# Moving small steps within the hand-written order of a float32 decoder layer: square sum, rotary, attention and weight-difference steps

## The chip, the cores and the metric

The kernel runs on one core of a Trainium2 chip. A core has five engines that each work through their own queue of instructions in order: TensorE (PE in the profile, with PEld for its weight loads), VectorE (DVE), ScalarE (ACT), GpSimd (POOL) and SyncE (SP), which here issues most transfers. They are tied together by semaphores only. The metric is device time of one execution in microseconds (us); the change is judged by the median of several executions against the kernel before.

## The reference: what is computed

One decoder layer in float32 on 520 rows: 512 of a prompt and 8 single rows of a sample group that has its own caches. d_model is 2048, the hidden width of the feed-forward 5632.

```python
h = rmsnorm(x, g_mix_pre)
proj = h @ w_in                          # q | k | v | B | C | u | gate_a | gate_b
a = attention(rope(q), rope(k), v)       # window 128, 16 heads over 2 key heads, a sink per head
b_out = cb * dwconv3(cc * cu)
merged = sigmoid(ga + b0) * (a @ w_attn_branch) + sigmoid(gb + b1) * (b_out @ w_conv_branch)
x = x + rmsnorm(merged @ w_o, g_mix_post)
up, gt = split(rmsnorm(x, g_ffn_pre) @ w_ffn_up)
x = x + rmsnorm((gelu(dwconv3(up) + bias) * gt) @ w_ffn_down, g_ffn_post)
x = x + sigmoid(x @ w_ple_gate) * (p @ w_ple)
```

## The kernel before

Activations lie feature-major: 128 features on the partitions, 520 rows along the free side in two halves of 260. A projection is worked off in **units**. A unit makes a 2 by 2 block of results (two column tiles of 128, two halves of 260 rows) with seven products in place of eight, in the manner of Strassen and Winograd: the weights and the rows enter as sums and differences of blocks. There are 116 units in seven **sets**: units 0 to 31 are the input projection (in it 2 to 5 are q, 6 to 17 the convolution's C, u and B, 18 to 31 gates), 32 to 39 w_o, 40 to 83 the up projection, 84 to 107 the down projection in three sets, 108 to 115 the last gate. Between the input projection and w_o stand the two branch projections (L967 to L999), and between w_o and the up projection the p projection.

**Float32 out of a faster type.** In the first unit of a set (`first_unit`, L866) TensorE multiplies float32 directly. In all others (`unit`, L897) each product is made of three matmuls in the reduced type float32r: high times high, high times low, low times high. A product j (0 to 6) has two halves h, so a unit has 14 **steps** i = 2j + h. For each step ScalarE writes the high part of the weights (`v_hi`, L1063) and VectorE the low part (`v_lo`, L1656), into a ring of four slots. Both run four steps ahead of TensorE: ScalarE's high part for step i + 4 waits until TensorE has used step i (`v_used`).

**VectorE's order.** `unit` at L1794 is one loop over the 14 steps. In step i it issues, in this order: the low part for step i + 4; in the second unit of a set (the one after `first_unit`) at i = 0, 3, 5, 8 two low parts of the rows (`o_low`, L1742); at i = 4 and 5 the weight difference s4; at 8 and 9 s1 and at 10 and 11 s3 of the next unit's weights; at 12 and 13 s2; then the set's own work, `evac(u, i)`. At i = 9 alone `evac` stands ahead of the rest. `evac` holds, for every set, the three adds of `sums` (L1822): at 7 the add "c11" after product 3, at 9 the add "c22" (L1831) after product 4, at 11 the add "c12" after product 5. It also holds the work of the stage: rotary (`sine`, `cosine`, `turn_q`), the convolution, attention of the prompt (`masked`, `shifts`, `probabilities`, `attention_out`) and of the sample rows (`sample_max` to `sample_out`).

**What TensorE waits for.** Product 6 accumulates in the bank that c22 reads, so it waits for c22 (`banks_free`, L849, j = 6). Each step waits for its low part. `between(u)` (L820) places TensorE's small work in a unit: key -1 is ahead of product 0, key j behind product j. That is `rotate` (the rotary matmul; both rotations of a unit use one bank, so the second waits for the first one's `sine`), `turn` (transposes of the probabilities), `scores`, `values`, and the same for the sample rows. Attention of the prompt runs in 16 parts; unit u in `ATT` scores and exponentiates a part, unit u in `TURN` transposes it and multiplies it with v. Units 19 to 30 do both, and gate units also take a sigmoid at i = 0 and 1.

**The start.** ScalarE squares each of the 16 row blocks and scales it (L1042, L1044), VectorE sums the squares into `sqacc1` (L1449). TensorE makes k and v from the scaled rows as they come (L724). The sum over partitions is two matmuls with a matrix of ones (`square_sum`, L707); from it VectorE and ScalarE make the inverse root (L1438, L1441, L1035), VectorE scales all row blocks with it (`h_row`, L1455) and builds the first differences (t1, s1, s3, t2, s2), and unit 0 can go on.

Of the kernel before, what the change touches and what calls it, by code (L numbers as in the profile page):

```python
# [8 lines left out]
KD = D // P  # L9
TP, TS = 512, 8  # L10
T = TP + TS
HALF = T // 2
# [13 lines left out]
U_O, N_O = 32, KD // 2  # L26
# [56 lines left out]
def build(nc, sstream, x_in, p_in, chan_in, sinkp_in, sinks_in, cstate_in, fstate_in,  # L83
# [5 lines left out]
    with ExitStack() as ctx:  # L89
# [610 lines left out]
        def _(pe):  # L700
# [3 lines left out]
            def x_half(k, h):  # L704
                return raw4[:, 2 * (k // KH) + h, k % KH, :]

            def square_sum():  # L707

                pe.wait_ge(sq_added, KD - 1)
                pe.wait_ge(pool_set, 3)  # L710
                for h in range(2):
                    mm = pe.matmul(pair[1][:, h, 0:HALF], ones[:, :],
                                   sqacc1[:, h * HALF:(h + 1) * HALF], start=True, stop=True)
                mm.then_inc(sum_ready, 1)

            for k in range(KD):
                if k == KD - 4:
                    square_sum()
                pe.wait_ge(x_rdy, k + 1)
                for n, w in enumerate(quarter_of(k)[:2]):  # L720
                    if k % KH == 0:
                        pe.wait_ge(s_rdy[0][2 * n + k // KH], 16)
                    for h in range(2):
                        mm = pe.matmul(pair[2 + n][:, h, 0:HALF], w[:, quarter_of(k)[2]], x_half(k, h),  # L724
                                       start=k == 0, stop=k == KD - 1, skip_group_check=True)
                mm.then_inc(kv_used, 1)
            def rotate(r):

                u = U_Q + r // 2
                if r < KA:  # L730
                    for n in ((c11_out, c12_out), (c22_out, c21_out))[r % 2]:
                        pe.wait_ge(n, u + 1)
                    src = d_h[u % 2][:, r % 2, :]
                else:
                    src = k_in
                pe.wait_ge(kv_out, 2)
                if r:
                    pe.wait_ge(rope_sin, r)
                for h in range(2):
                    mm = pe.matmul(pair[2][:, h, 0:HALF], rotm[:, :],  # L740
                                   src[:, h * HALF:(h + 1) * HALF], start=True, stop=True)
                mm.then_inc(rope_rot, 1)
# [77 lines left out]
            def between(u):  # L820

                if u - 1 in range(U_Q, U_CONV):
                    r = 2 * (u - 1 - U_Q)
                    return {-1: lambda: rotate(r), 1: lambda: rotate(r + 1)}
                if u == U_CONV + 1:
                    return {0: v_turn, 1: lambda: rotate(KA)}
                if u == U_CONV + 3:
                    return {0: sample_scores}
                if u == U_CONV + 4:
                    return {-1: sample_turn, 3: sample_values}  # L830
                here = {}
                if u in TURN or u in ATT:
                    here[-1] = lambda: (turn(TURN[u]) if u in TURN else None,
                                        scores(ATT[u]) if u in ATT else None)
                if u in TURN:
                    here[2] = lambda: values(TURN[u])
                if u == LAST:
                    here[4] = lambda: turn(ATT[u])
                    here[5] = lambda: values(ATT[u])
                return here  # L840
# [578 lines left out]
        def _(dve):  # L1419
# [374 lines left out]
            def unit(u, evac, last):  # L1794

                n = s_of(u, 0)
                ahead = 16 if u == U_O - 1 else 14 if last and u != U_UP - 1 else 18
                for i in range(14):
                    if i == 9:
                        evac(u, i)  # L1800
                    if i + 4 < ahead:
                        v_low(n + i + 4)
                    if is_first(u - 1) and i in (0, 3, 5, 8):
                        o_low(set_of(u), {0: 3, 3: 4, 5: 5, 8: 6}[i])
                    if i in (4, 5):
                        s4(u, i - 4)
                    if i in (8, 9) and u not in (U_O - 1, U_UP - 1):
                        s1(u + 1, i - 8)
                    if i in (10, 11) and u not in (U_O - 1, U_UP - 1):
                        s3(u + 1, i - 10)  # L1810
                    if i in (12, 13) and not last:
                        s2(u + 1, i - 12)
                    if i != 9:
                        evac(u, i)

            def by(s, evac, first=None):
                u0, n, _ = SETS[s]
# [69 lines left out]
            def h_evac(u, i):  # L1887
                d, k = d_h[u % 2], kind(u)
                if U_Q < u <= U_CONV:
# [4 lines left out]
                        cosine(r)  # L1894
                    if i == 2:
                        turn_q(r)
                    if i == 3:
                        sine(r + 1)
                        cosine(r + 1)
                    if i == 6:  # L1900
                        turn_q(r + 1)
# [38 lines left out]
                    if i == 8:  # L1940
                        sample_prob()
                if u == U_CONV + 4:
                    if i == 1:
                        sample_turned()
                    if i == 8:
                        sample_out()
                if u in ATT:
                    if i in (0, 1):
# [2 lines left out]
                        shifts(ATT[u])  # L1951
                    if i == 6:
                        probabilities(ATT[u])
                if u in TURN and i == 7:
                    attention_out(TURN[u])
                if u == LAST and i == 12:
                    attention_out(ATT[u])
# [390 lines left out]
```

## Time and profile before

| | before |
|---|---|
| median of 3 runs | 2798.61 us (2797.02 to 2798.67) |
| the profiled execution: its own time | 2798.67 us |
| its span, first to last instruction | 2796.1 us |
| TensorE busy | 2697.9 us |
| VectorE busy | 2294.1 us |
| ScalarE busy | 1416.9 us |
| mean granted TensorE clock | 0.987 |

The span is what the trace covers; 2.6 us of the execution lie around it. Busy times overlap, so they don't add up. TensorE's matmuls are pipelined: one of the 128x260 matmuls takes 0.28 us from start to end, but the next one starts 0.12 us later. In the same way the next VectorE operation on 128x512 elements starts 0.60 us after one that lasts 0.68 us. Intervals below are from start to start where a queue is full.

### The profile page before, as it was taken

How to read it: one execution, taken by the hardware profiler on the slowest of the kernel's cores; microseconds unless marked ns; L12 is line 12 of the kernel's file. 1: busy time of each engine (PE TensorE's matmuls, PEld its weight loads, DVE VectorE, ACT ScalarE, POOL GpSimd, SP SyncE). 2: the span in 40 equal slices, each digit the busy share in tenths (PEclk: the TensorE clock that was granted, in tenths of full speed). 3: DMA queues.
4: the chain of work that ended last, by engine and by line, in shares of the span. 5: the costliest groups of instructions: out<-in, count | busy, mean ns of one | idle time of the engine just before them, and what ended most of it. 6: DMA issues, size and time to landing. Idle time of an engine off the chain costs nothing. (4 is left out here: it accounts for less than half of the span.)

```text
span 2796.1 us, 55643 instructions
## 1 busy us (share of the span) xinstructions
PE 2697.9 (96%) x21199; PEld 2619.9 (94%) x21199; DVE 2294.1 (82%) x4039; ACT 1416.9 (51%) x2511; POOL 30.3 (1%) x52
## 2 busy tenths in 40 slices
PE   7999999999999999989999999999999999999799
PEld 6999999999999989879999999999998999989599
DVE  6988888777754598798888888888888788899988
ACT  5444455666652255545555555555554454445354
POOL 0000000000000000000000000000000000000000
PEclk9999999999999999999999999999999999999799
DMA  5333333333353422542323233333334342425343
GB/s 187 133 127 115 107 115 113 116 122 125 116 175 136 162 91 90 196 150 102 135 102 130 107 123 115 116 122 109 129 106 160 119 153 91 140 85 171 123 186 123
DMA packets 119157, 357.89 MB, mean 128 GB/s; under 512 B 13097, under 2 KB 37297, under 8 KB 116384
## 3 DMA queue, kind: packets, MB, share of 16 engines
q1 hardware_dynamic: 116944, 350.19, 35.6%
q0 software_dynamic: 2048, 5.68, 0.6%
q8 instruction: 82, 1.34, 0.2%
q14 instruction: 83, 0.68, 0.1%
HBM read 311.74 MB, written 45.32 MB: 128 GB/s over the span
## 5 line engine op out<-in xcount | busy, mean ns | idle before, releaser
L915 PE MATMUL pair<-o_hi,v_hi 128*128 128x260 f32 x6006 | 1715.0, 286 | 39.5 <-DVE v_lo L1656 11.7
L915 PE MATMUL pair<-o_hi,v_lo 128*128 128x260 f32 x6006 | 1699.2, 283 | 0.0
L1063 ACT ACTIVATE v_hi<-s_raw 128x512 fp32r<-128x512 f32 (+1 forms) x1380 | 855.3, 625 | 1008.1 <-PE pair L915 824.5
L915 PE MATMUL pair<-lo,v_hi 128*128 128x260 f32 x4290 | 1215.3, 283 | 0.0
L1656 DVE TENSOR_TENSOR v_lo<-s_raw,v_hi 128x512 fp32r<-128x512 f32 (+1 forms) x1380 | 934.5, 681 | 333.6 <-ACT v_hi L1063 285.7
L915 PEld LDWEIGHTS pair<-o_hi,v_hi 128*128 128x128 f32 x6006 | 1133.0, 189 | 64.3 <-issue 32.3
L915 PEld LDWEIGHTS pair<-o_hi,v_lo 128*128 128x128 f32 x6006 | 1135.1, 189 | 0.0
L915 PEld LDWEIGHTS pair<-lo,v_hi 128*128 128x128 f32 x4290 | 809.8, 189 | 0.3
L915 PE MATMUL pair<-lo_E,v_hi 128*128 128x260 f32 x858 | 243.2, 283 | 0.0
L915 PE MATMUL pair<-lo_A,v_hi 128*128 128x260 f32 x858 | 241.9, 282 | 0.0
L1063 ACT ACTIVATE v_hi<-s_one 128x512 fp32r<-128x512 f32 (+1 forms) x218 | 135.9, 626 | 192.8 <-PE pair L915 187.0
L915 PEld LDWEIGHTS pair<-lo_E,v_hi 128*128 128x128 f32 x858 | 161.6, 188 | 0.1
L915 PEld LDWEIGHTS pair<-lo_A,v_hi 128*128 128x128 f32 x858 | 161.3, 188 | 0.0
L1703 DVE TENSOR_TENSOR s_raw<-s_raw,s_raw 128x512 f32<-128x512 f32 (+1 forms) x232 | 156.0, 675 | 0.0
L1676 DVE TENSOR_TENSOR s_one<-s_raw,s_raw 128x512 f32<-128x512 f32 (+1 forms) x232 | 155.8, 675 | 0.0
L1684 DVE TENSOR_TENSOR s_raw<-s_raw,s_raw 128x512 f32<-128x512 f32 (+1 forms) x232 | 155.2, 674 | 0.0
L1694 DVE TENSOR_TENSOR s_raw<-s_one,s_raw 128x512 f32<-128x512 f32 (+1 forms) x232 | 155.1, 674 | 0.0
L1656 DVE TENSOR_TENSOR v_lo<-s_one,v_hi 128x512 fp32r<-128x512 f32 (+1 forms) x218 | 146.7, 675 | 5.2 <-ACT v_hi L1063 1.8
L892 PE MATMUL pair<-raw,s_raw 128*128 128x260 f32 x508 | 116.5, 385 | 5.0 <-DVE y_sb L1831 1.8
L892 PEld LDWEIGHTS pair<-raw,s_raw 128*128 128x128 f32 x508 | 94.7, 190 | 24.0 <-issue 2.8
L987 PE MATMUL pair<-br_hi,v_lo 128*128 128x260 f32 x512 | 103.2, 283 | 0.0
L987 PE MATMUL pair<-br_lo,v_hi 128*128 128x260 f32 x512 | 103.0, 283 | 0.0
(209 smaller groups left out, 2077.8 us busy)
## 6 DMA issues: line engine op xcount, KB each, us to landing
s_raw<-in_sstream SPq DMA_DIRECT2D x472, 512.0 KB, 4.7
s_raw<-in_sstream SPq DMA_DIRECT2D x32, 384.0 KB, 3.4
f_scr<-fo SPq DMA_DIRECT2D x88, 130.0 KB, 1.8
g_scr<-d_h SPq DMA_DIRECT2D x16, 520.0 KB, 2.7
g_in<-g_scr SPq DMA_DIRECT2D x32, 260.0 KB, 2.7
x_scr<-y_sb SPq DMA_DIRECT2D x8, 1040.0 KB, 3.9
raw<-f_scr SPq DMA_DIRECT2D x7, 1040.0 KB, 4.9
raw<-in_x SPq DMA_DIRECT2D x4, 1040.0 KB, 6.4
```

Source lines behind the costliest of these rows:

```text
L892: mm = pe.matmul(out, w[:, kk * P:kk * P + P], src[:, k, :], start=j in (0, 1, 3) and k == 0, stop=k == nk - 1, skip_group_check=True)
L915: mm = pe.matmul(out, wt[:, slot, kk * P:kk * P + P], r[:, k, :], start=j in (0, 1, 3) and k == 0 and n == 0, stop=k == nk - 1 and n == 2, ...
L987: mm = pe.matmul(pair[2 + p][:, half, 0:HALF], wt[:, slot, kk * P:kk * P + P], r[:, k, half * HALF:(half + 1) * HALF], start=k == 0 and i ...
L1063: nc.scalar.activation(v_hi[:, n % 4, 0:width], src, ACT.Copy).then_inc(v_hi_rdy, 1)
L1656: dve.tensor_tensor(v_lo[:, n % 4, 0:width], src, v_hi[:, n % 4, 0:width].bitcast(f32), ALU.subtract).then_inc(v_lo_rdy, 1)
L1676: dve.tensor_tensor(w_src(u, 1, h), quarter(u, 2, h), quarter(u, 3, h), ALU.add)\
L1684: dve.tensor_tensor(quarter(u, 2, h), quarter(u, 0, h), quarter(u, 2, h), ALU.subtract)\
L1694: dve.tensor_tensor(quarter(u, 0, h), w_src(u, 1, h), quarter(u, 0, h), ALU.subtract)\
L1703: dve.tensor_tensor(quarter(u, 1, h), quarter(u, 1, h), quarter(u, 0, h), ALU.subtract)\
```

## The change

Five edits. The square sum goes behind the k and v matmuls of all 16 row blocks. The second rotary matmul of a unit goes from behind product 1 to behind product 0, and its `sine` from step 3 to step 2. The sample rows' transposes go from the head of unit 10 to behind product 5 of unit 9, their value matmuls from behind product 3 to behind product 1 of unit 10, and the two copies on VectorE with them. The prompt's `values` go from behind product 2 to behind product 1, and `attention_out` from step 7 to step 5. In VectorE's loop s1 and s3 go one step ahead, and the special place of `evac` at step 9 goes away: it follows the low part and s3 there, as in all other steps.

```diff
-            def square_sum():
-                pe.wait_ge(sq_added, KD - 1)
-                ...
             for k in range(KD):
-                if k == KD - 4:
-                    square_sum()
                 pe.wait_ge(x_rdy, k + 1)
...
+            pe.wait_ge(sq_added, KD - 1)
+            pe.wait_ge(pool_set, 3)
+            for h in range(2):
+                mm = pe.matmul(pair[1][:, h, 0:HALF], ones[:, :],
+                               sqacc1[:, h * HALF:(h + 1) * HALF], start=True, stop=True)
+            mm.then_inc(sum_ready, 1)
...
-                    return {-1: lambda: rotate(r), 1: lambda: rotate(r + 1)}
+                    return {-1: lambda: rotate(r), 0: lambda: rotate(r + 1)}
...
-                    return {0: sample_scores}
+                    return {0: sample_scores, 5: sample_turn}
                 if u == U_CONV + 4:
-                    return {-1: sample_turn, 3: sample_values}
+                    return {1: sample_values}
...
-                    here[2] = lambda: values(TURN[u])
+                    here[1] = lambda: values(TURN[u])
...
                 for i in range(14):
-                    if i == 9:
-                        evac(u, i)
                     if i + 4 < ahead:
                         v_low(n + i + 4)
...
-                    if i in (8, 9) and u not in (U_O - 1, U_UP - 1):
-                        s1(u + 1, i - 8)
-                    if i in (10, 11) and u not in (U_O - 1, U_UP - 1):
-                        s3(u + 1, i - 10)
+                    if i in (7, 8) and u not in (U_O - 1, U_UP - 1):
+                        s1(u + 1, i - 7)
+                    if i in (9, 10) and u not in (U_O - 1, U_UP - 1):
+                        s3(u + 1, i - 9)
                     if i in (12, 13) and not last:
                         s2(u + 1, i - 12)
-                    if i != 9:
-                        evac(u, i)
+                    evac(u, i)
...
                     if i == 2:
                         turn_q(r)
+                        sine(r + 1)
                     if i == 3:
-                        sine(r + 1)
                         cosine(r + 1)
...
                 if u == U_CONV + 4:
-                    if i == 1:
+                    if i == 0:
                         sample_turned()
-                    if i == 8:
+                    if i == 4:
                         sample_out()
...
-                if u in TURN and i == 7:
+                if u in TURN and i == 5:
                     attention_out(TURN[u])
```

## Rows read from the trace of the kernel before

**Rows 1.** The page's busy times: us, share of the span, instructions.

```profile
PE 2697.9 (96%) x21199; PEld 2619.9 (94%) x21199; DVE 2294.1 (82%) x4039; ACT 1416.9 (51%) x2511; POOL 30.3 (1%) x52
```

**Rows 2.** TensorE's waits by releaser: us in total, times, longest us.

```profile
PE pair L915 <- DVE v_lo L1656: 11.7, 9, 4.4
PE pair L915 <- DVE d_h L1831: 9.5, 14, 2.4
PE pair L915 <- DVE y_sb L1831: 5.0, 4, 2.0
PE pair L915 <- DVE g_half L1831: 2.4, 1, 2.4
PE pair L915 <- DVE d_sb L1831: 1.3, 1, 1.3
```

**Rows 3.** Timeline of the start: start us, us, engine, line, operation, [idle before].

```profile
26.48 0.70 DVE L1449 TENSOR_TENSOR sqacc<-sqacc,sq_a 128x520 f32<-128x520 f32 x1 [0.45 <-ACT sq_a L1042]
...
31.57 1.04 PE L712 MATMUL pair<-sqacc,ones 128*128 128x260 f32 x4
...
32.45 7.18 PE L724 MATMUL pair<-raw,s_raw 128*128 128x260 f32 x32
32.65 0.70 DVE L1438 TENSOR_SCALAR nv_a<-pair 128x520 f32<-128x520 f32 x1 [5.46 <-PE pair L712]
...
45.54 3.77 PE L892 MATMUL pair<-raw,s_one 128*128 128x260 f32 x16 [2.32 <-DVE s_one L1676]
```

**Rows 4.** Timeline of unit 26, an attention unit in the gates, three engines.

```profile
643.56 0.63 ACT L1063 ACTIVATE v_hi<-s_raw 128x512 fp32r<-128x512 f32 x1 [2.94 <-PE pair L915]
...
647.55 1.07 ACT L1205 ACTIVATE pT_sb<-pair 128x512 f32<-128x512 f32 x2
...
647.70 0.39 PE L915 MATMUL pair<-o_hi,v_hi 128*128 128x260 f32 x1
...
653.97 0.69 DVE L1656 TENSOR_TENSOR v_lo<-s_raw,v_hi 128x512 fp32r<-128x512 f32 x1 [3.03 <-ACT v_hi L1063]
...
660.41 0.68 DVE L1676 TENSOR_TENSOR s_one<-s_raw,s_raw 128x512 f32<-128x512 f32 x1
661.01 0.42 DVE L1831 TENSOR_TENSOR d_h<-pair,d_h 128x260 f32<-128x260 f32 x1
661.35 0.68 DVE L1656 TENSOR_TENSOR v_lo<-s_raw,v_hi 128x512 fp32r<-128x512 f32 x1
...
661.48 0.39 PE L915 MATMUL pair<-o_hi,v_hi 128*128 128x260 f32 x1 [0.44 <-DVE d_h L1831]
```

**Rows 5.** Timeline of unit 54, in the up projection: steps 9 to 12.

```profile
1512.77 0.63 ACT L1063 ACTIVATE v_hi<-s_raw 128x512 fp32r<-128x512 f32 x1 [0.81 <-PE pair L915]
...
1513.21 0.42 DVE L1831 TENSOR_TENSOR g_half<-pair,g_half 128x260 f32<-128x260 f32 x1
...
1515.45 0.29 PE L915 MATMUL pair<-o_hi,v_hi 128*128 128x260 f32 x1
```

**Rows 6.** Timeline of unit 4, with rotary: product 1's first matmul, the first sine.

```profile
145.50 0.28 PE L915 MATMUL pair<-o_hi,v_hi 128*128 128x260 f32 x1
...
145.55 0.69 DVE L1483 TENSOR_TENSOR rope_s<-pair,sin 128x520 f32<-128x520 f32 x1
```

**Rows 7.** Timeline of unit 13: the add c22 and product 6's first matmul.

```profile
354.50 0.42 DVE L1831 TENSOR_TENSOR d_h<-pair,d_h 128x260 f32<-128x260 f32 x1
...
355.61 0.29 PE L915 MATMUL pair<-o_hi,v_hi 128*128 128x260 f32 x1
```

**Rows 8.** Timeline of unit 9, the sample rows' scores: step 8's low part, product 6.

```profile
267.79 0.69 DVE L1656 TENSOR_TENSOR v_lo<-s_raw,v_hi 128x512 fp32r<-128x512 f32 x1 [1.41 <-ACT v_hi L1063]
...
271.21 0.39 PE L915 MATMUL pair<-o_hi,v_hi 128*128 128x260 f32 x1 [2.42 <-DVE d_h L1831]
```

**Rows 9.** Timeline of unit 31, the last with attention: transposes behind product 4.

```profile
783.11 1.06 PE L806 MATMUL pair<-ident,s_sb 128*128 128x128 f32 x8 [1.79 <-DVE a_st L1598]
```

**Rows 10.** Windows: us, busy us (instructions) of PE, PEld, DVE, ACT, POOL; clock, DMA, GB/s.

```profile
1022.00:1027.00 5.00, 4.82 (x28) 4.83 (x29) 5.00 (x11) 1.52 (x3) 0.00 (x0) 0.67 0.31 119
```

More of the change, by code:

```diff
@@ L705, in x_half @@
                 return raw4[:, 2 * (k // KH) + h, k % KH, :]
-            def square_sum():
-                pe.wait_ge(sq_added, KD - 1)
[L710 to L714, printed above, removed]
             for k in range(KD):
-                if k == KD - 4:
-                    square_sum()
                 pe.wait_ge(x_rdy, k + 1)
```

## The prediction

> **What bounds the kernel now.** I read the page's busy times first: TensorE is busy for 2697.9 of 2796.1 us [rows 1]. So at most 98 us can be won, and whatever makes TensorE wait inside a unit is paid in full, unless it takes the place of another wait. Then TensorE's waits by releaser [rows 2]. What the reader is to see: beside the low parts (v_lo) it is one small add, c22 at L1831, that TensorE waits for in 14 + 4 + 1 + 1 = 20 units, 18.2 us together. Product 6 needs that add. Then the timelines of single units, with one question: how long before product 6's first matmul does c22 end (its slack)? I made that difference for all 109 units that aren't the first of a set. In units 18 to 30 it is 0.05, and also in 1, 9, 33, 41, 85, 93, 101 and 109 (up to 0.13): there the add decides. It is 0.69 to 1.15 in 2, 7, 13 and 16 [rows 7], about 1.1 in the six shorter units 102 to 107, and 1.66 to 2.25 in 77 others, of which [rows 5] is one: 1515.45 less 1513.21 + 0.42. Unit 31 has 4.1. Everything in the change that touches VectorE's steps 7 to 9 has to be held against this list.
>
> **The c22 add at step 9.** Before, VectorE does in steps 7 to 9: low part, c11; low part, s1; c22. After: low part, s1, c11; low part, s1; low part, s3; c22. So three operations on 128x512 stand ahead of c22 that stood behind it: one s1, one low part and one s3. A step from s1 to c22 takes 661.01 - 660.41 = 0.60 us [rows 4], and each of the three has this size: 3 x 0.60 = 1.8 us later, where VectorE's queue is full. The total work of VectorE is unchanged; only the add comes later.
>
> Units 18 to 30. VectorE is full from the low part at 653.97 to the add [rows 4]; it started there because ScalarE released it, and ScalarE's own chain starts at 643.56, when TensorE has used step 0. So c22 comes a fixed time after step 0 of its own unit, and TensorE waits on it: 13 x 1.8 = 23.4 us. (Unit 18's wait isn't in the list of waits, but its product 6 starts 0.06 after the add like the others.)
>
> Units 13 and 16, 2 and 7. VectorE is full there too, but c22 ended 0.69, 0.69, 1.08 and 1.15 us early; for unit 13 that is 355.61 - 354.92 [rows 7]. The wait is 1.8 less the slack plus the 0.05 that a released matmul needs: 1.2 + 1.2 + 0.8 + 0.7 = 3.9 us.
>
> Second units of the sets. 1, 33, 41, 85 and 109 wait on c22 already, with VectorE full behind the low parts of the rows: 5 x 1.8 = 9.0 us. In 93 and 101 VectorE idled 0.99 and 0.79 us behind c11, which takes in the early s1: 1.2 and 0.9 (operations of 0.47 there); and in 101 a later wait of 0.6 on VectorE goes, since VectorE is no later than before: 1.6 together. In unit 9 the idle 1.41 us [rows 8] takes in the s1 as well: 1.2.
>
> The 77 units with slack. There VectorE isn't full, and c22 is bound by the high part for step 13, which ends at 1512.77 + 0.63 = 1513.40 [rows 5]. Low part and s3 (0.60 each), then the add of 0.42: 1515.02 to 1515.07, against a need at 1515.45. Some 0.4 is left (0.2 in the tightest), so these cost nothing. That cover is thin: where it is missed by 0.1 in all 77, it is 8 us. In 102 to 107 the same sum ends within 0.05 of the need; I take 0, and 0.1 each as a bound. s1 one step earlier also waits for its weights earlier. SP issues the last quarter of them behind the low part of step 13 of the unit before the last, nearly a unit ahead, so neither that nor SP's own wait shows.
>
> **The values behind product 1.** They wait for both copies of the transposed probabilities. These end at 647.55 + 1.07 = 648.62, while product 1 is through at 647.70 [rows 4]: TensorE would stand 0.95 us, with products 2 to 6 queued behind. In units 19 to 30 this isn't added. c22 is tied to step 0, and TensorE runs into its wait at product 6 anyway; the 0.95 is taken from that wait, which would be 0.44 + 1.8. Step for step nothing in ScalarE's chain asks for products 2 and 3 sooner. In units 14 and 17 (no sigmoid, slack 1.66) nothing swallows it: the copies end 0.73 us late, 2 x 0.75 = 1.5 us. `attention_out` at step 5 finds its matmuls done and costs nothing by itself. In unit 31 it is a gain: the transposes behind product 4 waited 1.79 for it [rows 9], and now wait for the probabilities, which end one low part and one copy sooner and start one copy later: -0.6, after the 0.95 is swallowed by the same wait.
>
> **The second rotation behind product 0.** It needs the first `sine` out of its bank. Product 0 ends where product 1 starts, 145.50; the sine ends at 145.55 + 0.69 = 146.24 [rows 6]. TensorE stands 0.8 us, in units 3 to 6: 3.2 us. The sine moved to step 2 makes a later operation of VectorE earlier, which nobody waited for.
>
> **The sample rows.** ss_prob is ready before c22 in unit 9, so the four transposes fall into TensorE's wait there, and unit 10 loses them: about -0.4. With the 1.2 above, unit 9 and 10 cost +0.8. The value matmuls only change place, their copy is ready.
>
> **The square sum.** The sum of squares is there at 26.48 + 0.70 = 27.2, but TensorE is behind and reaches the place at 31.57 [rows 3], so no wait is removed. After, the 32 matmul instructions of row blocks 12 to 15 stand ahead of it, 7.0 us from start to start of what follows. L1438 starts at 32.65, when the sum is out, with all of VectorE's start behind it (inverse root, row scaling, s1). TensorE already waits on that chain: 2.32 us for s_one at 45.54, with the k and v matmuls done long before [rows 3]. So the four blocks hid the inverse root, and after nothing does: +7.0 us.
>
> **The sum.** 23.4 + 3.9 + 9.0 + 1.6 + 1.5 - 0.6 + 3.2 + 0.8 + 7.0 = 49.8 us.
>
> **The clock.** In unit 33 a wait of 1.97 us (the longest of the y_sb row [rows 2]) was followed by a window with a granted clock of 0.67, a mix of full and the lower of the two levels (2.4 and 1.2 GHz) [rows 10]; the unit and the next took 1.65 us more than their like. Unit 9 with 2.42 and unit 31 with 1.79 saw no fall. Eight places (1, 9 and the second units) now wait longer: between 0 and 8 x 1.65 = 13 us; I take three, 5 us, since like waits before fell in some and not in others.
>
> Against the execution's own 2798.67 us (its span and 2.6 around it; the median is 0.06 less) this is 2798.7 + 49.8 + 5 = 2853.5 us.
>
> **The rivals.**
>
> *The clock falls in every attention unit.* After, these units have two waits, 0.95 and 1.25, every 26.5 us. If one of them drops the clock each time, 13 x 1.65 = 21 us come on top: 2875. Against it: 12 waits of 0.44 and one of 1.79 left the clock at full. The Trainium skill, page "TensorE: Matmul & The Clock Gate", section "HAM oscillation — how this bites in real kernels", says that a loop that waits in each turn can go back to half rate in each turn, and that half of the throttled time is lost. No stretch of this trace repeats such a fall. Chance 0.07.
>
> *The thin cover tears.* If the low part or s3 at step 9 takes 0.3 us more than I read off, the 77 units wait 0.3 each past their 0.4, or the first part of that: up to 23 us, 2876. For it: only 0.2 to 0.4 is left. Against: VectorE's times repeat to 0.02. Chance 0.08.
>
> *The add isn't what holds product 6.* The releaser is inferred. If product 6 waited for something else that ends near c22, such as its own low part, the add could slip without a price: what stays is 7.0 + 3.2 + 1.5, with a wait or two: 2811. Against it: a slack of 0.05 in 13 units in a row. Chance 0.07.
>
> *Faster.* The low part for step 13 no longer stands behind the add and a step's s1. If TensorE's waits on low parts, 11.7 us [rows 2], all came from there, they would go, and if the idle time before s_one took in the late square sum, the kernel would be at 2787. It decides in a unit only where c22 has more than 1.8 us of slack and a low part has none. Against it: where TensorE waits for low parts, c22 has none either, and these waits stand ahead of step 13. Chance 0.03.
>
> **How the numbers follow.** The forecast has the other 0.75; with its own bounds (clock 0 to 13, the shorter units 0 to 0.6, ±3 for the readings off single rows) it spans 2845 to 2866. The range takes in most of the two rivals above and part of the one below: 2838 to 2872. A change under 0.2%, 5.6 us, can't be told from none. Slower 0.96, same 0.01, faster 0.03.
>
> **What would show it.** Right: TensorE's waits on L1831 grow from 18.2 to some 50 us, in units 18 to 30 the period goes from 24.7 to 26.5 us, and new waits appear on the copies of the probabilities (15 times, 0.75 to 0.95) and on the rotary sine (4 times, 0.8); L1438 starts near 39.7; the up projection keeps its period of 20.17. Wrong: a period in the up projection above 20.2, attention units at 24.7 or above 27, or an L1438 that starts before 35.

## The result, and the profile after

The changed kernel takes 2859.39 us (median of four runs, 2858.37 to 2863.52), the kernel before 2797.82 us (four runs, 2795.78 to 2798.67). The ratio is 1.0224, with a 95% interval of 1.0206 to 1.0242: slower by 61.6 us. The forecast was 2853.5 us in a range of 2838 to 2872, and slower. The profiled execution after took 2858.77 us, with a span of 2856.3 us and a mean granted clock of 0.980. So the span grew by 60.2 us.

The page's busy times after, beside [rows 1]:

```profile
PE 2711.4 (95%) x21199; PEld 2633.2 (92%) x21199; DVE 2300.2 (81%) x4039; ACT 1418.6 (50%) x2511; POOL 30.3 (1%) x52
```

The number of instructions is the same on every engine. TensorE is busy 2711.4 - 2697.9 = 13.5 us longer with the same 21199 matmuls, and idle for the other 60.2 - 13.5 = 46.7 us. This isn't the split into clock and waits, for which the forecast had 5 and 49.8: a matmul at the lower clock counts as busy, but so do small stands between matmuls, and these changed as well (see `x3_values`). In units 18 to 30 the busy time grew by 318.68 - 313.93 = 4.75 us, although the clock cost 9.1 us there. The split is made below from the starts of the units.

TensorE's waits by releaser after, beside [rows 2] (c11, c22 and c12 now lie seven lines higher, the square sum's matmuls are at L719, the other lines below have moved up by three, four or seven):

```profile
PE pair L911 <- DVE d_h L1824: 31.2, 19, 3.6
PE pair L811 <- ACT pT_sb L1201: 12.3, 16, 0.8
...
PE pair L911 <- DVE v_lo L1652: 11.8, 9, 4.5
...
PE pair L911 <- DVE y_sb L1824: 9.6, 5, 3.8
...
PE pair L888 <- DVE raw L1451: 5.7, 1, 5.7
...
PE pair L911 <- DVE g_half L1824: 4.2, 1, 4.2
PE pair L911 <- DVE d_sb L1824: 3.1, 1, 3.1
PE pair L736 <- DVE rope_s L1479: 2.9, 4, 0.7
...
PE pair L764 <- DVE ss_sb L1539: 2.1, 1, 2.1
```

The waits on c22 (L1824) are 31.2 + 9.6 + 4.2 + 3.1 = 48.1 us, from 18.2. The waits on low parts are what they were, 11.8 after 11.7. New are the waits on the copies of the probabilities (16, 0.8 at most; before there was one of 0.3), on the rotary sine (4, 0.7), on the sample rows' probabilities (2.1) and on the scaled rows in unit 0 (5.7).

Timeline of the start, beside [rows 3], and of units 4, 9 and 13, beside [rows 6 to 8]:

```profile
26.60 0.70 DVE L1445 TENSOR_TENSOR sqacc<-sqacc,sq_a 128x520 f32<-128x520 f32 x1 [0.44 <-ACT sq_a L1038]
...
37.52 1.04 PE L719 MATMUL pair<-sqacc,ones 128*128 128x260 f32 x4
...
38.59 0.70 DVE L1434 TENSOR_SCALAR nv_a<-pair 128x520 f32<-128x520 f32 x1 [11.29 <-PE pair L719]
...
51.49 3.77 PE L888 MATMUL pair<-raw,s_one 128*128 128x260 f32 x16 [1.28 <-DVE s_one L1672]
...
155.70 0.69 DVE L1479 TENSOR_TENSOR rope_s<-pair,sin 128x520 f32<-128x520 f32 x1
...
156.54 1.12 PE L736 MATMUL pair<-d_h,rotm 128*128 128x260 f32 x4 [0.72 <-DVE rope_s L1479]
...
284.91 0.58 PE L764 MATMUL pair<-ident,ss_sb 104*128 104x104 f32 x4 [2.08 <-DVE ss_sb L1539]
...
286.45 0.39 PE L911 MATMUL pair<-o_hi,v_hi 128*128 128x260 f32 x1 [0.96 <-DVE d_h L1824]
...
372.87 0.42 DVE L1824 TENSOR_TENSOR d_h<-pair,d_h 128x260 f32<-128x260 f32 x1
...
373.34 0.39 PE L911 MATMUL pair<-o_hi,v_hi 128*128 128x260 f32 x1 [1.01 <-DVE d_h L1824]
```

VectorE now stands 11.29 us for the square sum, with the squares added up at 27.3. The inverse root begins at 38.59 in place of 32.65, and the rest of the start with it: TensorE works on s_one at 51.49, before at 45.54. In unit 4 TensorE stands for the sine. In unit 9 it stands for the sample rows' probabilities, and then once more for c22. In unit 13 product 6 starts 0.05 after the add, where it had 0.69 to spare.

Timeline of unit 26, beside [rows 4]. It starts at 682.87, the next one at 709.37:

```profile
684.61 0.63 ACT L1059 ACTIVATE v_hi<-s_raw 128x512 fp32r<-128x512 f32 x1 [2.95 <-PE pair L911]
...
688.60 1.07 ACT L1201 ACTIVATE pT_sb<-pair 128x512 f32<-128x512 f32 x2
...
689.72 1.09 PE L811 MATMUL pair<-pT_sb,v_tok 128*64 128x256 f32 x8 [0.82 <-ACT pT_sb L1201]
...
695.02 0.69 DVE L1652 TENSOR_TENSOR v_lo<-s_raw,v_hi 128x512 fp32r<-128x512 f32 x1 [3.04 <-ACT v_hi L1059]
...
702.06 0.68 DVE L1672 TENSOR_TENSOR s_one<-s_raw,s_raw 128x512 f32<-128x512 f32 x1
702.66 0.68 DVE L1652 TENSOR_TENSOR v_lo<-s_raw,v_hi 128x512 fp32r<-128x512 f32 x1
703.26 0.68 DVE L1680 TENSOR_TENSOR s_raw<-s_raw,s_raw 128x512 f32<-128x512 f32 x1
703.87 0.42 DVE L1824 TENSOR_TENSOR d_h<-pair,d_h 128x260 f32<-128x260 f32 x1
...
704.34 0.39 PE L911 MATMUL pair<-o_hi,v_hi 128*128 128x260 f32 x1 [1.78 <-DVE d_h L1824]
```

From the high part of ScalarE to c22 it is 703.87 - 684.61 = 19.26 us; in [rows 4] it is 661.01 - 643.56 = 17.45. The difference is 1.81, the three operations. One sees them in the order forecast: s1, low part, s3, add. The copies end at 689.67 and the values wait 0.82 for them. The wait on c22 is 1.78, which is 0.46 less than 0.44 + 1.8: the values' wait has been taken out of it in part, and `x3_values` shows where the rest of it went.

Timeline of the next unit, 27, TensorE from product 6 on:

```profile
730.83 0.39 PE L911 MATMUL pair<-o_hi,v_hi 128*128 128x260 f32 x1 [1.80 <-DVE d_h L1824]
...
731.65 0.42 PE L911 MATMUL pair<-o_hi,v_lo 128*128 128x260 f32 x1
731.87 0.42 PE L911 MATMUL pair<-o_hi,v_hi 128*128 128x260 f32 x1
...
734.69 0.33 PE L911 MATMUL pair<-lo,v_hi 128*128 128x260 f32 x1
```

Windows after (us, busy PE, PEld, DVE, ACT, POOL, clock, DMA share, GB/s): unit 26, unit 27, a stretch behind product 6's start in unit 27, units 18 to 30 together, and 40 units of the up projection:

```profile
682.87:709.37 26.50, 23.89 (x195) 22.43 (x193) 18.72 (x42) 16.17 (x32) 1.42 (x2) 1.00 0.31 110
709.37:737.38 28.01, 25.39 (x195) 23.93 (x193) 18.71 (x42) 16.17 (x32) 1.42 (x2) 0.94 0.30 105
...
731.00:734.50 3.50, 3.50 (x19) 3.50 (x20) 2.35 (x5) 0.63 (x1) 0.00 (x0) 0.55 0.51 195
...
466.30:818.40 352.10, 318.68 (x2491) 300.09 (x2489) 246.43 (x540) 205.46 (x410) 17.58 (x25) 0.97 0.31 108
1331.80:2138.50 806.70, 806.70 (x6723) 806.70 (x6722) 702.37 (x1241) 437.05 (x760) 0.00 (x0) 1.00 0.33 118
```

Units 26 and 27 have the same waits (0.82 and 1.8) and the same instructions. In 26 the clock stays full; in 27 it falls to the lower level (1.2 GHz) behind the wait on c22, and matmuls start 0.22 us apart, from 731.65 to 734.69, in place of 0.12. That makes unit 27 longer by 1.51 us. It is so in units 20, 21, 23, 25, 27 and 29. Units 18 to 30 took 319.49 us before. The first of the two windows below shows that; the second shows the 40 units of the up projection in the kernel before, which take the same 806.70 us as after:

```profile
445.75:765.24 319.49, 313.93 (x2490) 292.58 (x2489) 242.91 (x539) 204.18 (x410) 17.58 (x25) 1.00 0.34 119
1276.30:2083.00 806.70, 806.70 (x6722) 806.70 (x6721) 702.24 (x1241) 437.27 (x760) 0.00 (x0) 1.00 0.33 117
```

Timeline of unit 54, beside [rows 5]: this unit keeps its 20.17 us, with 1570.94 - (1570.14 + 0.42) = 0.38 us of slack left from 1.82.

```profile
1568.26 0.63 ACT L1059 ACTIVATE v_hi<-s_raw 128x512 fp32r<-128x512 f32 x1 [0.81 <-PE pair L911]
...
1568.93 0.69 DVE L1652 TENSOR_TENSOR v_lo<-s_raw,v_hi 128x512 fp32r<-128x512 f32 x1
1569.54 0.69 DVE L1680 TENSOR_TENSOR s_raw<-s_raw,s_raw 128x512 f32<-128x512 f32 x1
1570.14 0.42 DVE L1824 TENSOR_TENSOR g_half<-pair,g_half 128x260 f32<-128x260 f32 x1
...
1570.94 0.29 PE L911 MATMUL pair<-o_hi,v_hi 128*128 128x260 f32 x1
```

### The profile page after: what moved, and what is told of

The parts are those of the page before. It is cut to its first block and busy times, and to the rows that moved or that the text cites. A ratio compares the mean times of both kernels' runs of the same rounds, so it can differ in the third digit from the quotient of the medians.

```text
span 2856.3 us, 55643 instructions
## 1 busy us (share of the span) xinstructions
PE 2711.4 (95%) x21199; PEld 2633.2 (92%) x21199; DVE 2300.2 (81%) x4039; ACT 1418.6 (50%) x2511; POOL 30.3 (1%) x52
## 5 line engine op out<-in xcount | busy, mean ns | idle before, releaser
L911 PE MATMUL pair<-o_hi,v_hi 128*128 128x260 f32 x6006 | 1720.4, 286 | 67.1 <-DVE d_h L1824 31.2
```

What stands on the lines that cost most here:

```text
L911: mm = pe.matmul(out, wt[:, slot, kk * P:kk * P + P], r[:, k, :], start=j in (0, 1, 3) and k == 0 and n == 0, stop=k == nk - 1 and n == 2, ...
```

## The experiments

All kernels start from the kernel before unless said otherwise. Ratios are to the kernel before in the same set of runs, whose median was 2797.59 us for `x1_sum` to `x4_rotate`, 2797.96 for `x6_add` to `x9_early`, and 2797.29 for `x5_values_order`, `x10_rest`, `x11_final` and `x12_sum6`. "Start of product 6" is counted from the start of its unit, in units 19 to 30: +19.66 before, +21.47 after the change.

### The parts of the change, one at a time

**x2_order**: VectorE's loop alone.

```diff
-                    if i == 9:
-                        evac(u, i)
...
-                    if i in (8, 9) and u not in (U_O - 1, U_UP - 1):
-                        s1(u + 1, i - 8)
-                    if i in (10, 11) and u not in (U_O - 1, U_UP - 1):
-                        s3(u + 1, i - 10)
+                    if i in (7, 8) and u not in (U_O - 1, U_UP - 1):
+                        s1(u + 1, i - 7)
+                    if i in (9, 10) and u not in (U_O - 1, U_UP - 1):
+                        s3(u + 1, i - 9)
...
-                    if i != 9:
-                        evac(u, i)
+                    evac(u, i)
```

> The kernel before, with the changed order in VectorE's loop alone (c22 behind the low part and s3 of step 9, s1 and s3 one step ahead). Theory (the late add is the price): 13 x 1.8 in units 18 to 30, 3.9 in units 2, 7, 13 and 16, 10.6 in the second units, 1.2 in unit 9: +39 us without the clock, and the up projection keeps its period of 20.17 us. In units 19 to 30 the wait before product 6 is a single one of 0.44 + 1.8 = 2.25 us. On the clock two theories: if it is the pair of waits of the changed kernel (0.82 and 1.79 us in one unit) that lets it fall, no fall in units 18 to 30 and 2840 to 2848 us; if one long wait does it as well, falls in about half of them or more at 1.5 us each, 2850 to 2858 us. Rival (the add isn't what holds product 6): 2798 to 2805 us.

Measured: 2850.7 us, ratio 1.0192 (1.0175 to 1.0209), 53.1 us slower. Product 6 starts at +21.46; the waits on c22 are 56.0 us together, longest 3.6. The window of units 18 to 30:

```profile
453.50:805.45 351.95, 322.93 (x2490) 301.60 (x2488) 246.37 (x540) 204.21 (x410) 17.59 (x25) 0.97 0.31 108
```

It is 351.95 - 319.49 = 32.5 us longer, as in the changed kernel. Six of these units are 28.0 long with the lower clock behind the wait, and the others 26.5. There is one wait of 2.24 here and none ahead of it. So most of the loss is this edit, and the clock's fall doesn't need the values' wait beside it.

**x1_sum**: the square sum behind row block 15.

```diff
             for k in range(KD):
-                if k == KD - 4:
-                    square_sum()
                 pe.wait_ge(x_rdy, k + 1)
...
                 mm.then_inc(kv_used, 1)
+            square_sum()
```

> The kernel before, with the square sum behind all k and v matmuls alone. Theory: the four row blocks (7.0 us) stop hiding the inverse root; everything of VectorE's start moves by 6 to 7 us, and the unit after the first keeps 5.3 of it as in the changed kernel: 2803 to 2805 us. Rival (TensorE's idle time before s_one takes it in): 2798 us, L1438 late but s_one not.

Measured: 2804.77 us, ratio 1.0025 (1.0015 to 1.0034), 7.2 us slower. The inverse root starts here:

```profile
38.80 0.70 DVE L1438 TENSOR_SCALAR nv_a<-pair 128x520 f32<-128x520 f32 x1 [11.82 <-PE pair L712]
```

The edit costs about what the four row blocks ahead of it take, 7.0 us. Unit 1 starts at 81.34. In the eight kernels that leave the start alone, the one before among them, it starts at 73.34 to 75.57, and at 80.87 to 81.34 in the three with the late sum.

**x3_values**: the values behind product 1 and `attention_out` at step 5.

```diff
-                    here[2] = lambda: values(TURN[u])
+                    here[1] = lambda: values(TURN[u])
...
-                if u in TURN and i == 7:
+                if u in TURN and i == 5:
                     attention_out(TURN[u])
```

> The kernel before, with values behind product 1 and attention_out at step 5 alone. Theory (the wait of 0.82 to 0.95 on the copies is taken from the wait on c22, which is only 0.44 here): +0.4 to 0.5 in each of units 19 to 30, +0.75 in 14 and 17, -0.6 in unit 31: +6 us, 2803 to 2805 us, with c22's slack above 0.05 in units 19 to 30. Rival (nothing is taken in): 12 x 0.95 + 1.5 - 0.6 = +12 us, 2810 us. Rival (all is hidden): 2799 us.

Measured: 2797.65 us, ratio 0.9999 (0.999 to 1.0009): no difference. The theory's 6 us were wrong, and the rival that all of it is hidden was right in units 19 to 30. In 14 and 17 the wait costs 0.73 and 0.72, and unit 31 gives 0.7 back. In the stretch from 440 to 790 us the waits of TensorE are these, and none on c22 is listed any more:

```profile
PE pair L815 <- ACT pT_sb L1205: 11.1, 14, 0.8
PE pair L806 <- DVE s_sb L1590: 0.4, 1, 0.4
```

Product 6 starts at +19.66 as before, and the units keep their 24.68. I had set a wait of 0.95 against one of 0.44 and charged the difference. But 0.44 isn't all that stood there. The last matmul of product 5 counts as busy for 0.28 us, while the next could start 0.12 after it. So a listed 0.44 loses about 0.60. And there were small stands in products 3 to 5 that are listed nowhere. In unit 26 products 1 and 2, with the values behind one of them, took 7.00 us before and take 7.89 here; products 3 to 5, with the wait for product 6, took 9.68 and take 8.79. So the values' wait costs 0.89 and gives 0.89 back, some 0.6 of it from the listed wait and 0.3 from the small stands. Product 6 still starts 0.05 behind c22. The prediction had this edit at nothing in these units, for the better reason: c22 is tied to step 0.

**x4_rotate**: the second rotation behind product 0, its sine at step 2.

```diff
-                    return {-1: lambda: rotate(r), 1: lambda: rotate(r + 1)}
+                    return {-1: lambda: rotate(r), 0: lambda: rotate(r + 1)}
...
                         turn_q(r)
+                        sine(r + 1)
                     if i == 3:
-                        sine(r + 1)
```

> The kernel before, with the second rotation behind product 0 and its sine at step 2 alone. Theory: TensorE waits 0.72 us on the first sine in units 3 to 6, each such unit is 0.8 to 0.95 us longer, 22.8 in place of 21.92: +3.2 to 3.8 us, 2801 to 2802 us, less than a measurement can tell, so the trace decides. Rival (the slack of the unit takes it in): the units stay at 21.92.

Measured: 2800.32 us, ratio 1.0011 (1.0001 to 1.0021), 2.7 us slower. Units 3 to 6 take 0.95 us more each, in the changed kernel as well: 3.8.

**x10_rest**: the other way round, the changed kernel with VectorE's loop as it was before.

```diff
+                    if i == 9:
+                        evac(u, i)
...
-                    if i in (7, 8) and u not in (U_O - 1, U_UP - 1):
-                        s1(u + 1, i - 7)
-                    if i in (9, 10) and u not in (U_O - 1, U_UP - 1):
-                        s3(u + 1, i - 9)
+                    if i in (8, 9) and u not in (U_O - 1, U_UP - 1):
+                        s1(u + 1, i - 8)
+                    if i in (10, 11) and u not in (U_O - 1, U_UP - 1):
+                        s3(u + 1, i - 10)
...
-                    evac(u, i)
+                    if i != 9:
+                        evac(u, i)
```

> The changed kernel with VectorE's loop as before (steps 7 to 9 undone, all other edits kept). Theory (the edits add up, and the order in VectorE's loop is most of the loss): +7.2 from the square sum, +2.7 from the rotations, 0 from values, -0.4 from the sample rows' transposes: 2806 to 2809 us, product 6 at +19.65 in units 19 to 30, hardly a fall of the clock there. Rival (the values' wait counts once the rest is changed): 2815 us.

Measured: 2807.3 us, ratio 1.0035 (1.0022 to 1.0049), 10.0 us slower, as expected. Product 6 starts at +19.66, with no fall of the clock in units 18 to 30. The 10.0 of this kernel and the 53.1 of `x2_order` make 63.1, against the 61.6 of the whole change. So the two parts add up to within 1.5 us. The sample rows' moves have no run of their own, but this kernel shows them without the late add: units 9 and 10 are 0.30 and 0.09 us shorter than before.

**x5_values_order**: `x2_order` and `x3_values` together.

```diff
-                    here[2] = lambda: values(TURN[u])
+                    here[1] = lambda: values(TURN[u])
...
-                if u in TURN and i == 7:
+                if u in TURN and i == 5:
...
-                    if i != 9:
-                        evac(u, i)
+                    evac(u, i)
```

(with the other lines of `x2_order` too.)

> The kernel before, with the order in VectorE's loop and the move of values and attention_out together. Theory (the values' wait is taken from the wait on c22): as the order alone, product 6 at +21.46 in units 19 to 30, +0.4 in 14 and 17, -0.7 in unit 31: 2848 to 2854 us, some six falls of the clock in units 18 to 30. Rival for the clock (two waits in a unit let it fall more often than one): ten or more falls, 2856 us or more; fewer, because each wait is shorter: 2845 us or less.

Measured: 2851.69 us, ratio 1.0195 (1.0179 to 1.021). Product 6 starts at +21.47, and six units fall again; units 18 to 30 take 352.20 us. Two waits of 0.82 and 1.8 cost what one of 2.24 costs.

### How many operations stand ahead of the add

Three kernels split the loop's edit, and one goes the other way.

**x9_early**: only s1 and s3 one step ahead, the special place of `evac` kept. One operation more, an s1, stands ahead of c22.

```diff
-                    if i in (8, 9) and u not in (U_O - 1, U_UP - 1):
-                        s1(u + 1, i - 8)
-                    if i in (10, 11) and u not in (U_O - 1, U_UP - 1):
-                        s3(u + 1, i - 10)
+                    if i in (7, 8) and u not in (U_O - 1, U_UP - 1):
+                        s1(u + 1, i - 7)
+                    if i in (9, 10) and u not in (U_O - 1, U_UP - 1):
+                        s3(u + 1, i - 9)
```

> The kernel before, with only s1 and s3 one step ahead; the step 9 work keeps its place ahead of the low part. Theory: one s1 more stands ahead of c22, product 6 at +20.25 in units 19 to 30: 13 x 0.6, 5 x 0.6 in the second units, 0 in 9 and 93 (idle time takes it in): +11 us and a few us of clock, 2808 to 2816 us. Rival (the early differences make room later and win): 2795 us or less.

**x6_add**: only the special place of `evac` goes. Two more stand ahead, s1 and a low part.

```diff
-                    if i == 9:
-                        evac(u, i)
...
-                    if i != 9:
-                        evac(u, i)
+                    evac(u, i)
```

> The kernel before, with only the place of the step 9 work changed: c22 behind the low part and the s1 of step 9; s1 and s3 stay at steps 8 to 11. Theory (each operation of VectorE put ahead of c22 costs its 0.60 us where the queue is full, whichever it is): product 6 starts 1.2 us later in its unit, at +20.85 in place of +19.65 in units 19 to 30; units of slack 1.68 to 1.83 keep theirs above 0.4. 13 x 1.2, some 1.3 in 13 and 16 and 0.3 in 2 and 7, 7 to 8 in the second units, 1.2 in unit 9: +26 us without the clock, 2824 us; with some falls of the clock at 1.5 each up to 2838 us. Rival (the early s1 is what hurts): 2798 us.

**x8_s1**: both halves of s1 at step 9, behind the add. One fewer stands ahead.

```diff
-                    if i in (8, 9) and u not in (U_O - 1, U_UP - 1):
-                        s1(u + 1, i - 8)
+                    if i == 9 and u not in (U_O - 1, U_UP - 1):
+                        both_halves(s1, u + 1)
```

> The kernel before, with both s1 at step 9 behind c22 and the low part, so one s1 less ahead of c22. Theory (the same price the other way): c22 0.60 us sooner where the queue is full; the waits of units 18 to 30 end when their loss of 0.6 or less is gone, and another wait (low parts of steps 11 and 12) takes over early: -0.4 to -0.6 in each of 13 units, -0.6 in 1, 33, 41, 85, 109 and 9: 2787 to 2790 us. Rival (the hidden small waits on low parts ahead of product 6 hold the unit at 24.68): 2794 us. Rival (the later s1 comes late for the high parts of step 2 of the next unit): above 2798 us.

Measured, with the kernel before and `x2_order` for comparison:

| | more ahead of c22 | median us | ratio (95%) | start of product 6 | units with a fall, 18 to 30 |
|---|---|---|---|---|---|
| x8_s1 | -1 | 2784.29 | 0.9953 (0.9939 to 0.9966) | +19.06 | 0 |
| before | 0 | 2797.96 | 1 | +19.66 | 0 |
| x9_early | 1 | 2808.16 | 1.0038 (1.0023 to 1.0054) | +20.26 | 0 |
| x6_add | 2 | 2825.27 | 1.0097 (1.0082 to 1.0113) | +20.86 | 0 |
| x2_order | 3 | 2850.7 | 1.0192 (1.0175 to 1.0209) | +21.46 | 6 |

The windows of units 18 to 30 in `x8_s1`:

```profile
443.98:755.85 311.87, 311.70 (x2491) 292.56 (x2489) 242.28 (x538) 204.25 (x410) 17.57 (x25) 1.00 0.36 121
```

in `x9_early`:

```profile
446.44:773.69 327.25, 313.95 (x2491) 292.69 (x2489) 243.43 (x540) 204.19 (x410) 17.57 (x25) 1.00 0.34 116
```

and in `x6_add`:

```profile
451.82:786.95 335.13, 313.98 (x2491) 292.72 (x2489) 244.72 (x540) 204.20 (x410) 17.57 (x25) 1.00 0.33 113
```

Each operation is 0.60 us, on either side of the kernel before: 327.25 - 319.49 = 7.8 = 13 x 0.60, and 335.13 - 319.49 = 15.6 = 13 x 1.20. The third step breaks the line: 352.0 - 335.1 = 16.8, which is 13 x 0.60 and six falls of 1.5. The medians of `x9_early` and `x6_add` together are 10.2 + 27.3 = 37.5 us over, that of `x2_order` 53.1. Of the 15.6 between, the six falls are 9.1. In the traces another 3.3 are in units 2, 7, 8, 11, 13, 14, 16 and 17, where one or two operations are covered by slack and a third isn't. The rest is in the start and in single falls of the clock elsewhere, which differ from one execution to the next.

`x8_s1` came out 13.7 us faster, better than expected. In units 18 to 30 it is 7.6 us, the ladder's price, and no wait of TensorE is listed there any more. TensorE counts as busy for 311.70 of 311.87 us, but small stands count as busy too: product 6 still starts 0.05 behind c22 in units 19 to 30, and product 5 of unit 26 takes 3.13 us where it takes 3.02 in `x3_values`. So it isn't shown that the stage is at its floor. The rest comes from the second units of the sets, 0.6 each from the add, and more in 33, 85 and 109, where the clock was higher in this execution than in that of the kernel before.

### Other places for what was moved

**x12_sum6**: the square sum ahead of row block 10 in place of 12.

```diff
-                if k == KD - 4:
+                if k == KD - 6:
                     square_sum()
```

> The kernel before, with the square sum ahead of row block 10 in place of 12 alone. Theory (each row block ahead of the sum costs its 1.8 us of TensorE as long as the sum of squares is there): L1438 at 28.5 to 29.5 in place of 32.65, the next unit's start 3 to 4 us sooner: 2793 to 2795 us. Rival (TensorE's time is full until s_one and nothing is won): 2798 us.

Measured: 2792.66 us, ratio 0.9985 (0.9975 to 0.9994), 4.6 us faster. The inverse root starts at 28.40, and unit 1 at 70.74 (75.57 before):

```profile
28.40 0.70 DVE L1438 TENSOR_SCALAR nv_a<-pair 128x520 f32<-128x520 f32 x1 [1.24 <-PE pair L712]
```

**x7_best**: `x8_s1` and `x12_sum6`, with the change's `attention_out` and sample rows.

```diff
-                if k == KD - 4:
+                if k == KD - 6:
...
-                    return {0: sample_scores}
+                    return {0: sample_scores, 5: sample_turn}
                 if u == U_CONV + 4:
-                    return {-1: sample_turn, 3: sample_values}
+                    return {1: sample_values}
...
-                    if i in (8, 9) and u not in (U_O - 1, U_UP - 1):
-                        s1(u + 1, i - 8)
+                    if i == 9 and u not in (U_O - 1, U_UP - 1):
+                        both_halves(s1, u + 1)
...
-                if u in TURN and i == 7:
+                if u in TURN and i == 5:
```

(and `sample_turned` at step 0, `sample_out` at step 4.)

> The kernel before, with what the readings recommend: both s1 behind c22 at step 9, the square sum two row blocks sooner than before (ahead of row block 10), attention_out at step 5, and the sample rows' moves as in the change; values, rotations and the rest as before. Theory: -8 to -10 from s1, -4 from the start (L1438 near 28.5), -0.6 in unit 31, -0.4 to -1 in unit 9: 2782 to 2786 us. Rival (TensorE then stands at the sum, because the squares end at 27.2): the start wins 2 us or less, 2785 to 2789 us.

Measured: 2779.8 us, ratio 0.9938 (0.9924 to 0.9952). But the attention units take 24.31 us, not the 24.08 of `x8_s1`. TensorE's waits from 440 to 800 us have a row that `x8_s1` doesn't:

```profile
PE pair L915 <- DVE v_lo L1656: 4.1, 12, 0.3
```

The copy `attention_out` at step 5 stands ahead of a low part that TensorE is about to need. In the changed kernel the same copy cost nothing, since TensorE stood for c22 later anyway.

**x11_final**: as `x7_best`, with `attention_out` at step 5 in unit 31 alone.

```diff
-                if u in TURN and i == 5:
+                if u in TURN and i == (5 if u == LAST else 7):
```

> The combined kernel (both s1 behind c22, square sum ahead of row block 10, sample rows' moves), with attention_out at step 5 in unit 31 alone and at step 7 elsewhere. Theory (at step 5 attention_out stands ahead of the low part of step 11, for which TensorE then waits in 12 units: 24.31 in place of 24.08 us): 24.08 again, -2.8 us: 2776 to 2778 us. Rival: 2780 us.

Measured: 2779.1 us, ratio 0.9935 (0.9922 to 0.9949). The attention units are back at 24.08 and the waits on low parts are gone, but the total is only 0.7 us under `x7_best`, where the copy's 12 x 0.23 = 2.8 us were expected. The gain in the attention units is there, 12 x 0.23 us. But in the two profiled executions stretches that the edit doesn't touch are longer in `x11_final`: unit 1 starts 1.2 us later, unit 41 takes 26.1 us in place of 24.6 at a lower clock, and the stretch with unit 84 takes 1.9 more. What made these differ wasn't looked into. The two kernels can't be told apart by their times. Both beat the kernel before by 18 us, and this is what `x8_s1` and `x12_sum6` make alone: 13.7 + 4.6 = 18.3.

## Why the prediction was right

The time came out 5.9 us over the forecast of 2853.5 and well inside the range. Term by term, from the starts of the units in both traces (these include the clock, whose share is named):

| term | forecast | measured |
|---|---|---|
| c22 in units 18 to 30 | 23.4 | 32.6, of it 9.1 clock |
| c22 in 13, 16, 2, 7 | 3.9 | 4.1 |
| c22 in the second units, without 9 | 10.6 | 12.1 with the clock |
| values in 14 and 17 | 1.5 | 1.5 |
| unit 31 | -0.6 | -0.7 |
| rotation, units 3 to 6 | 3.2 | 3.8 |
| units 9 and 10 | 0.8 | 2.3, of it 1.5 clock |
| square sum | 7.0 | 5.3 to unit 1; 7.2 alone |
| units taken at nothing (8, 11, 103 to 106) | 0 | 0.9 |
| between the sets | not named | -1.8 |
| sum | 49.8 and 5 for the clock | 60.1 of the span's 60.2 |

**The add c22.** The step held in all of its parts. VectorE is full from step 7 to the add, each operation ahead of it is 0.60 us, and product 6 follows the add by 0.05. The ladder of four kernels beside the one before shows this, with nothing moved but VectorE's operations around c22. It refutes two rivals at once. That the add isn't what holds product 6 would have left `x6_add` and `x9_early` where the kernel before is. That the waits on low parts go would have to show in the v_lo row, which stayed at 11.8.

**The thin cover** held: 0.38 of slack in the up projection against a forecast of 0.4, and 806.70 us for 40 units in both kernels. Units 8 and 11 had been counted among those with slack, but VectorE is full in them: against 1.8, their slack of 1.71 and 1.76 was too little, and they took 0.20 and 0.19 more. 103 to 106 took 0.11 to 0.16 more each, a little over the bound of 0.1.

**The values, the sine, the sample rows.** The places and the numbers of the waits came as said (16 and 4, where 15 and 4 were forecast). The sine's 0.95 per unit was put at 0.8: it is the listed 0.72 and most of the rest is what a listed wait leaves out, as in `x3_values`. One split was wrong: the second wait of an attention unit was put at 1.25 and is 1.8. The product 6 start of +21.47 doesn't depend on it, but the argument on the clock did.

**The square sum.** TensorE was behind, so the move removes no wait and costs the four row blocks. The first step of the inverse root (L1438, L1434 after the change) starts at 38.59 in this execution and at 38.80 and 38.97 in the other two kernels with the late sum. 39.7 was forecast from a start of 32.65, which was the late side of what kernels with an untouched start show (31.46 to 32.67). For the same reason the 5.3 of the table is low: the trace of the kernel before has the latest start of unit 1 of all eight, 75.57. `x1_sum`'s 7.2 between medians is the better measure of the 7.0.

**The clock is the term that was mis-sized**: 5 us were taken, about 12 came. By the starts of the units it is 9.1 in the attention units, 1.5 in unit 9 and some 1.3 in the second units. The forecast put it at the eight places that wait longer, at 1.65 each. In two of them, 1 and 9, the clock fell behind the wait on c22, where before it had not. In 93 and 101 it fell as well, but ahead of product 6, behind waits on other adds that were as long before (2.85 after 2.84, 1.83 after 1.82), and it cost next to nothing: in unit 93 the wait on c22 is 0.33, where `x5_values_order` has 1.66 without a fall, and the units take 26.40 and 26.22 us. A fall ahead of a wait is taken out of that wait. But 6 x 1.51 = 9.1 us are in the attention units, which a rival with a chance of 0.07 had named. It came true for six of the thirteen. Only 9 of its 21 us came, and this is why the forecast was still near. The step that failed in it is the evidence against: that "12 waits of 0.44 and one of 1.79 left the clock at full" says nothing on thirteen of 1.8 in a row. It also had the second wait at 1.25. `x6_add` shows how near the edge was. With waits of 1.64 in the same units none fell, and with 2.24 (`x2_order`) or 0.82 and 1.80 six did. The Trainium skill, page "TensorE: Matmul & The Clock Gate", section "HAM oscillation — how this bites in real kernels", says of a loop with longer waits than these that it goes back to half rate in each turn, and that half of the throttled time is lost. The trace agrees on the loss (matmuls 0.22 apart where 0.12 is usual), but here it is not each turn: unit 26 stayed at 1.00 and unit 27 did not, with the same waits.

The -1.8 us between the sets are -1.3 from unit 39 to 41, -1.0 from 83 to 85 and +0.5 from 107 to 109. They say little of the change: `x1_sum`, `x3_values` and `x12_sum6`, whose edits don't touch these stretches, are 0.3 to 0.8 and 1.3 to 1.8 us shorter in the first two as well. The trace of the kernel before had long stretches there, and a fall of the clock in units 33 and 34 (1.5 us) that the five kernels with the same code there don't have. So parts of a single pair of traces are good to 1 or 2 us only.

What stays open is why unit 26 is spared and 27 isn't. No run was made for it.

## What to carry to other kernels

In an in-order queue that is full, the price of an operation is paid by whatever stands behind it. Count the operations that pass ahead of the one a bounding engine waits for, multiply by the interval at which the queue issues them, and look up the slack of each unit rather than of an average one. A wait that is cheap in itself gets dear where it repeats and drops TensorE's clock, so price a lengthened wait in a loop with the fall as well. And the ladder that shows a loss also points the other way: taking one more operation out from ahead of the add gave 13.7 us, 7.6 of it in the attention units, and asking the square sum as soon as the squares are there gave 4.6.

## What the runs showed of the hardware that wasn't expected

- With the same waits in each unit the clock fell in some and not in others: in 20, 21, 23, 25, 27 and 29 after the change, and in 6 of 13 as well in `x2_order` and `x5_values_order`. A fall cost 1.5 us each time in these units.
- A fall ahead of a wait on another engine costs next to nothing: in unit 93 it left 0.33 us of a wait that was 1.66 in `x5_values_order`, and the unit was 0.2 us longer.
- The same wait of 2.42 us in unit 9 left the clock full in the kernel before and was followed by a fall in `x3_values` (25.2 and 26.7 us for the unit), although nothing in or ahead of that unit's own order had been changed. So falls at single places can't be forecast to better than their 1.5 us.
- A listed wait understates what is lost by about 0.16 us: the last matmul ahead of it counts as busy for 0.28 us, while the next could have started 0.12 after it.
